# Expert-gate products from f32 to fp32r (gates split high and low, 64 blocks), with an own tile for the expert's activations and a new order of the index stage and of the last experts

## What is computed

```python
s1, s2 = scores of the query halves against keys1, keys2     # 128 keys each
top_s, pos = lax.top_k(v1[..., :, None] + v2[..., None, :], PEER_TOPK)
expert = i1 * PEER_KEYS + i2                # per token 8 heads x 16 experts
gate = softmax(top_s)
z = einsum('cd,ced->ce', x, u[expert])
act = gelu(z) * gate
out = einsum('ce,ced->cd', act, v[expert])
return rmsnorm(x + out, norm_final_g)
```

## Time and profile before

| | us |
|---|---|
| median of 3 runs | 2832.45 (2830.51 to 2834.54) |
| the profiled execution | 2833.08 |
| its span, first to last instruction | 2831.20 |
| TensorE busy | 2763.3 (98%) |
| DVE busy | 1814.0 (64%) |
| ACT busy | 1388.5 (49%) |
| POOL busy | 251.2 (9%) |
| TensorE's granted clock, mean share | 0.99 |
| read from HBM | 501.49 MB |

### The profile page before, as it was taken

One profiled execution on the slowest core, in us unless ns is written; L12 is line 12 of the kernel. 1 busy time (PEld: TensorE's weight loads), 2 busy tenths in 40 slices (PEclk: granted clock), 3 DMA queues, 4 the chain that ended last, 5 costly groups with the idle time before them and its releaser, 6 DMA issues.

```text
span 2831.2 us, 49456 instructions
## 1 busy us (share of the span) xinstructions
PE 2763.3 (98%) x15452; PEld 2414.6 (85%) x15452; DVE 1814.0 (64%) x2892; ACT 1388.5 (49%) x2016; POOL 251.2 (9%) x340
## 2 busy tenths in 40 slices
PE   8999999899999999999999999999999999999998
PEld 6888877788888888889999999888888888888886
DVE  6666655657986666578886666666664555555555
ACT  5454545545665444455555554555544444444444
POOL 0000000000000000000004997000000000000000
PEclk9999999999999999999999999999999999999999
DMA  6544454554554444555565454666665555555555
GB/s 245 188 148 167 159 178 150 169 202 144 172 166 164 156 156 141 181 196 184 185 207 174 159 160 153 219 210 214 210 205 179 193 193 193 192 193 193 193 192 191
DMA packets 153406, 514.70 MB, mean 182 GB/s; under 512 B 17040, under 2 KB 33680, under 8 KB 152208
## 3 DMA queue, kind: packets, MB, share of 16 engines
q1 hardware_dynamic: 131904, 482.54, 51.5%
q10 hardware_dynamic: 21456, 31.60, 3.1%
HBM read 501.49 MB, written 12.58 MB: 182 GB/s over the span
## 4 chain that ended last, share of the span: by engine, by line
PE 59%; DVE 1%; ACT 0%; issue 0%; DVEq 0%; POOL 0%; ACTq 0%; POOLq 0%
PE bank L482 12%; PE bank L2013 8%; PE bank L2014 8%; PE bank L2015 8%; PE bank L487 6%; PE bank L467 3%; PE bank L468 3%; PE bank L469 3%; PE bank L1988 2%; PE bank L522 1%; PE bank L521 1%; PE bank L520 1%; PE bank L1963 0%; DVE act L1027 0%; DVE big L1682 0%
## 5 line engine op out<-in xcount | busy, mean ns | idle before, releaser
L444 DVE TENSOR_TENSOR w_lo<-raw,w_hi 128x1024 fp32r<-128x1024 f32 x904 | 1098.3, 1225 | 827.5 <-ACT w_hi L435 822.7
L435 ACT ACTIVATE w_hi<-raw 128x1024 fp32r<-128x1024 f32 x904 | 953.5, 1059 | 1045.6 <-PE bank L2015 384.3
L482 PE MATMUL bank<-act,w_hi 128*128 128x512 f32 x3072 | 787.7, 398 | 4.5 <-ACT big L797 1.8
L482 PEld LDWEIGHTS bank<-act,w_hi 128*128 128x128 f32 x3072 | 554.4, 189 | 110.9 <-issue 5.5
L487 PEld LDWEIGHTS bank<-act,w_lo 128*128 128x128 f32 x3072 | 418.8, 190 | 31.1
L487 PE MATMUL bank<-act,w_lo 128*128 128x256 f32 x3072 | 427.8, 282 | 0.0
L2013 PE MATMUL bank<-w_hi,act 128*128 128x512 f32 x1024 | 399.5, 390 | 4.9 <-DVE act L1653 4.9
L2014 PE MATMUL bank<-w_lo,act 128*128 128x512 f32 x1024 | 399.1, 390 | 0.0
L2015 PE MATMUL bank<-w_hi,act 128*128 128x512 f32 x1024 | 399.1, 390 | 0.0
L467 PE MATMUL bank<-act,w_hi 128*128 128x256 f32 x912 | 261.6, 287 | 2.3 <-DVE w_lo L444 1.9
L469 PE MATMUL bank<-act,w_lo 128*128 128x256 f32 x912 | 259.4, 284 | 0.0
(11 more groups left out here) (276 smaller groups left out, 2344.8 us busy)
## 6 DMA issues: line engine op xcount, KB each, us to landing
raw<-in_stream SPq DMA_DIRECT2D x904, 512.0 KB, 3.3
big<-in_ukv ACTq DMA_DIRECT2D x16, 512.0 KB, 5.2
z_kept<-cst ACTq DMA_DIRECT2D x64, 128.0 KB, 3.2
cst<-z_kept ACTq DMA_DIRECT2D x64, 128.0 KB, 3.7
big<-in_x SPq DMA_DIRECT2D x2, 1024.0 KB, 9.5
big<-in_rows ACTq DMA_DIRECT2D x2, 1024.0 KB, 5.9
big<-in_rg_w ACTq DMA_DIRECT2D x1, 2048.0 KB, 8.1
x_kept<-big ACTq DMA_DIRECT2D x1, 2048.0 KB, 6.6
```

The source lines that it names most:

```text
L435: act.activation(w_hi[:, s, :], raw[:, s, :], ACT.Copy).then_inc(hi_ready, 1)
L444: dve.tensor_tensor(w_lo[:, s, :], raw[:, s, :], w_hi[:, s, :].bitcast(F32), ALU.subtract).then_inc(lo_ready, 1)
L482: pe.matmul(bank[:, :], w_hi[:, s, kk * P:(kk + 1) * P], act2[:, k, :, :].rearrange("p a n -> p (a n)"), start=(k == 0), stop=False)
```

## The change

- `u_gates` has 64 pairs instead of 32, `u_late` 32 instead of 64. Behind each of the 64 pairs, not behind each unit, stand the gate products of four tokens. `EARLY`, the number of z blocks stored to DRAM, rises from 64 to 96. 32 of them are fetched and multiplied in the late stage, 64 in the first 32 turns of the experts.
- The gate products are fp32r. The one-hot times gate is made twice, once with the gate's high part (rounded to fp32r by ACT into `gate_hi`) and once with the rest (`gate_lo`), both by DVE into `weighted`; two products accumulate. The plain one-hot of POOL is the stationary operand of both.
- DVE's order: both parts of tokens 0 and 1, split of unit 0, both parts of tokens 2 and 3, split of unit 1, `add_halves`. ACT: both splits, low half, one `keep_gates` of four tokens, Gelu, store.
- The experts' split activations get a tile of their own, `expert_act`, laid on the place of `weighted`. Experts 0 and 1 are split before the last late turn. TensorE's unit 0 of the first expert no longer waits for the end of ACT's and DVE's work; unit 1 waits for the last sum.
- Index stage: kw's transposes stand behind the first unit of the first query pair; KID is turned before CKV and copied first, and the scores wait for that copy alone. At the end: scores, rnn inputs of block 0, scores, rnn queries of block 0.
- Last two experts: token tile 0 for both, then tile 1 bank by bank (`last_experts`, `bank_done`). x is fetched early, into `big`. Tile 0 is normed and stored while TensorE works on tile 1. The scaling is shared: DVE one half of the columns, ACT the other after POOL has multiplied it with the gain. Six stores instead of four.

```diff
-         ("wqu", 4 * PH), ("u_decode", 2 * PH), ("u_gates", S // 8), ("u_late", NB // 2), ("v", NB)]
-EARLY = NB // 2
+         ("wqu", 4 * PH), ("u_decode", 2 * PH), ("u_gates", S // 4), ("u_late", NB // 4), ("v", NB)]
+EARLY = 3 * NB // 4
+LATE = NB - EARLY
...
+        with nc.sbuf_tensor("expert_act", [P, 2, 2, S], F32R) as expert_act:
+            pass
+        weighted = sb("weighted", [P, 4, 2, P], F32R)
+        with nc.sbuf_tensor("below_hot", [P, CONST["causal"][0]], F32), \
+                nc.sbuf_tensor("hot", [P, 4, P], F32R) as hot:
+            pass
...
         @block.gpsimd
-                    pool.tensor_scalar(hot[:, 1, s % 4, :], iota, idx8[:, s:s + 1], None, ALU.is_equal)\
+                    pool.tensor_scalar(hot[:, s % 4, :], iota, idx8[:, s:s + 1], None, ALU.is_equal)\
                         .then_inc(hot2, 1)
+            for t in range(TT):
+                pool.wait_ge(y_added, 4 * t + 2)
+                pool.tensor_tensor(OUT[:, t, 0:1024], XF[:, t, 0:1024], final_row[:, 0:1024], ALU.mult)\
+                    .then_inc(gained, 1)
...
         @block.scalar
+            act.wait_ge(ki_turned, 1)
+            act.activation(KIT, banks[2][:, 0:S], ACT.Copy).then_inc(ki_kept, 1)
             for k in range(RT):
...
-            for n in range(2):
-                index_relu(IH // 4 - 1, n)
+            index_relu(IH // 4 - 1, 0)
+            ahead(split_hi, act, "rnn", 0, 2, 0, units=(0,))
+            index_relu(IH // 4 - 1, 1)
...
+            act.activation(gate_hi.bitcast(F32R), slot_t[:, 2, :], ACT.Copy).then_inc(slots_kept, 1)
+            with act.Fori(0, S // 8) as i:
                 for n in range(2):
+                    for u in range(2):
+                        ahead(split_hi, act, "u_gates", i, 2, n, units=(u,))
                     act.wait_ge(unit_done, 2 * pair_of("u_gates", i, 2, n) + 2)
                     act.wait_ge(z_saved[n], i * 16 + (32 * PH + 1))
                     low_half(act, GZ[:, n, :], banks[2 + n])
+                    act.wait_ge(hot_used[3], i * 2 + n + 2)
+                    act.activation(G[:, :, bass.ds(i * 8 + 4 * n, 4)],
+                                   banks[n][:, :].rearrange("p (t b) -> p b t", t=4), ACT.Copy)\
+                       .then_inc(gate_kept[n], 1)
...
         @block.vector
+            step(dve.tensor_tensor(gate_lo, slot_t[:, 2, :], gate_hi, ALU.subtract))
+            step.wait()
+            with dve.Fori(0, S // 8) as i:
                 for n in range(2):
+                    for s in range(4):
+                        tok = i * 8 + (4 * n + s)
+                        dve.wait_ge(hot_used[s], i * 2 + n + 1)
+                        for part, weight in enumerate([gate_hi, gate_lo]):
+                            dve.tensor_scalar(weighted[:, s, part, :], iota, slot_t[:, 0, bass.ds(tok, 1)],
+                                              weight[:, bass.ds(tok, 1)], ALU.is_equal, ALU.mult).then_inc(hot1, 1)
+                        if s % 2:
+                            ahead(split_lo, dve, "u_gates", i, 2, n, units=(s // 2,))
                     add_halves(dve, GZ[:, n, :], banks[2 + n], block_of("u_gates", i, 2, n))
...
+            with dve.Fori(0, (EARLY - LATE) // 2) as i:
                 for n in range(2):
+                    next_expert(i, n)
+                    dve.wait_ge(z_back[n], i * 16 + (8 * LATE + 16))
+                    back = G[:, bass.ds(i * 2 + (LATE + n), 1), :].rearrange("p o n -> p (o n)")
+                    dve.tensor_tensor(back, GB[:, n, :], back, ALU.mult).then_inc(early_ready[n], 1)
...
         @block.tensor
             pe.wait_ge(ckv_kept, 2)
+            index_queries(0, 0, units=(0,))
+            pe.wait_ge(kwt_kept, 1)
+            for t in range(TT):
+                ins = pe.transpose(banks[3][:, t * P:(t + 1) * P], KWT[:, t * P:(t + 1) * P], ident)
+            ins.then_inc(kw_turned, 1)
+            index_queries(0, 0, units=(1,))
+            index_queries(0, 1)
...
+            pe.wait_ge(ki_kept, 1)
...
+            index_scores(IH // 4 - 1, 0)
+            rnn_inputs(0)
+            index_scores(IH // 4 - 1, 1)
+            rnn_queries(0)
...
+            with pe.Fori(0, S // 8) as i:
                 for n in range(2):
                     pe.wait_ge(gelu_ready[n], i + (2 * PH + 1))
+                    halves_out(pe, pair_of("u_gates", i, 2, n), n, banks[2 + n])
+                    pe.wait_ge(gate_kept[n], i + 1)
+                    for s in range(4):
+                        pe.wait_ge(hot1, i * 16 + (8 * n + 2 * s + 2))
+                        pe.wait_ge(hot2, i * 8 + (4 * n + s + 1) + 1)
+                        out_ap = banks[n][:, s * P:(s + 1) * P]
+                        pe.matmul(out_ap, hot[:, s, :], weighted[:, s, 0, :], start=True, stop=False)
+                        pe.matmul(out_ap, hot[:, s, :], weighted[:, s, 1, :], start=False, stop=True)\
+                          .then_inc(hot_used[s], 1)
...
+                    if first and u == 1:
+                        wait_summed(pe, block_of("u_late", LATE // 2 - 1, 2, 1))
...
+            for u in range(2):
+                for n in range(2):
+                    pe.wait_ge(el_ready, NB - 1 + n)
+                    pe.wait_ge(lo_ready, UNITS - 3 + 2 * n + u)
+                    for cc in range(2):
+                        last_experts(0, u, n, cc)
+            for u in range(2):
+                for cc in range(2):
+                    for n in range(2):
+                        last_experts(1, u, n, cc)
```

More of the change, by code:

```diff
@@ L305, in build @@
         final_ready = sem("final_ready")
-        xf_ready = [sem(f"xf_ready{t}") for t in range(TT)]
+        xf_ready = sem("xf_ready")
         x_saved = sem("x_saved")
@@ L833, in rnn_block @@
             def rnn_block(j, first=False):
-                ahead(split_hi, act, "rnn", j, 2, 0, units=(0,))
+                if not first:
+                    ahead(split_hi, act, "rnn", j, 2, 0, units=(0,))
                 act.wait_ge(unit_done, 2 * pair_of("rnn", j, 2, 0) + 2)
@@ new lines, in _, with final_squares @@
+            expert_hi(last * 2 + 2, 0, 2 * pair_of("v", last, 2, 0) + 2)
+            ahead(split_hi, act, "v", last, 2, 1, units=(0,))
+            expert_hi(last * 2 + 3, 1, 2 * pair_of("v", last, 2, 1) + 2)
+            ahead(split_hi, act, "v", last, 2, 1, units=(1,))
+            warm_root()
+            def final_squares(t, cb):
+                cols = slice(cb * 512, (cb + 1) * 512)
+                act.wait_ge(y_added, 4 * t + cb + 1)
+                act.activation(SQ[:, t, cols], XF[:, t, cols], ACT.Square,
+                               accum_out=ss4[:, 4 * t + cb:4 * t + cb + 1]).then_inc(fin_squares, 1)
@@ L1015, in _ @@
+            act.wait_ge(gained, 1)
+            act.wait_ge(fin_rstd, 1)
+            final_scale(0, slice(0, 1024))
+            final_squares(1, 2)
+            final_squares(1, 3)
+            final_root(1)
+            act.wait_ge(gained, 2)
+            act.wait_ge(fin_rstd, 2)
+            for q in range(2):
+                final_scale(1, slice(q * 512, (q + 1) * 512))
         @block.vector
@@ L1382, in _ @@
                     ahead(split_lo, dve, "qi", i, 2, n + 2)
-            for n in range(2):
-                index_sum(IH // 4 - 1, n)
+            index_sum(IH // 4 - 1, 0)
+            ahead(split_lo, dve, "rnn", 0, 2, 0, units=(0,))
+            index_sum(IH // 4 - 1, 1)
             for t in range(TT):
@@ L1423, in rnn_block @@
             def rnn_block(j, first=False):
-                ahead(split_lo, dve, "rnn", j, 2, 0, units=(0,))
                 if not first:
+                    ahead(split_lo, dve, "rnn", j, 2, 0, units=(0,))
                     rnn_gates(j - 1)
@@ L1676, in _ @@
[L1676 to L1684 removed]
+                dve.wait_ge(act_ready[n], LATE // 2 + 1)
@@ new lines, in _, with add_expert_bank @@
+            with dve.Fori((EARLY - LATE) // 2, NB // 2 - 2) as i:
+                for n in range(2):
+                    next_expert(i, n)
+            last = NB // 2 - 2
+            ahead(split_lo, dve, "v", last, 2, 0)
+            expert_lo(last * 2 + 2, 0, last * 2 + 3)
+            ahead(split_lo, dve, "v", last, 2, 1, units=(0,))
+            expert_lo(last * 2 + 3, 1, last * 2 + 4)
+            ahead(split_lo, dve, "v", last, 2, 1, units=(1,))
+            def add_expert_bank(t, cb):
+                dve.wait_ge(bank_done, 4 * t + cb + 1)
+                xs = XF[:, t, cb * 512:(cb + 1) * 512]
+                dve.tensor_tensor(xs, xs, banks[4 * t + cb][:, :], ALU.add).then_inc(y_added, 1)
@@ L1687, in _ @@
+            dve.wait_ge(y_added, 4)
+            dve.wait_ge(final_ready, 16)
+            final_rows(0, slice(1024, 2048))
+            add_expert_bank(1, 2)
+            add_expert_bank(1, 3)
+            final_mean(1)
+            final_reciprocal(1)
+            dve.wait_ge(y_added, 8)
+            for q in range(2):
+                final_rows(1, slice(1024 + q * 512, 1536 + q * 512))
```

(24 more changed lines are left out.)

227 lines of the change are left out of this document (116 added, 111 removed).

## The result

| | us |
|---|---|
| before, median of 5 runs beside it | 2832.55 (2830.51 to 2835.32) |
| after, median of 5 runs | 2848.18 (2846.38 to 2849.47) |
| ratio | 1.0052, 95% interval 1.0038 to 1.0067 |
| span of the profiled execution | 2847.66 (before 2831.20) |

The change makes the kernel 15.6 us slower, where 3.4 us on the profiled execution was forecast. The 2848.18 lies just above the upper end of the whole range, 2848, and 3 us above the forecast's own, 2845. The three gains came about as forecast, one of them larger; the gate part cost 34 us and not 19.6.

A forecast was written before the change was run, and what follows sets the result against it. TensorE, busy 98%, was taken to bound the kernel; gate part +19.6, into the experts -6.8, index end -4.6, index front 0, tail -4.8 give +3.4 us on 2833.08: 2836, range 2812 to 2848, the forecast's own 2827 to 2845.

The forecast's parts named there:

- The three gains: Forecast savings outside the gate part: into the experts -6.8 us, end of the index stage -4.6, tail -4.8.
- The products: Gate stage: each fp32r product of 128 columns costs TensorE 0.111 us, a block 0.93 as before, so fp32r alone brings nothing.
- Rival 2: Gate stage: load isn't the pace, products take 0.07 us, wait for DVE stays, pair 6.76; 2829 us; chance 0.09.
- rival 3: Gate stage: an fp32r product of 128 columns costs 0.22 us, like an f32 pair of records; pair 7.38; 2869; chance 0.08.
- rival 4: Gate stage: two one-hots per token cost DVE 0.07 us more each, 18 us in all; 2854; chance 0.07.
- The chain to the last token: Gate stage: unit 0's end through w_hi, w_lo and four one-hots takes 3.75 us; TensorE, there at 3.47, waits about 0.3.
- what stands behind the wait: Gate stage: loads aren't taken ahead of the wait, so two products and one for the next unit follow it, 0.33 us.
- Rival 1: Gate stage: DVE's last two tokens are in time, no wait, pair 6.53, in all -18.2 us; 2815; chance 0.18.
- Into the experts: Late stage to first expert: own tile lets unit 0 start at once, unit 1 waits some 0.3 us; -6.8 us.
- End of the index stage: Last score groups: rnn block between them removes two Relu-copy waits and the half clock behind; -4.6 us (bounds -3 and -5).
- the zero: Front of the index stage: earlier KIT copy offset by DVE's delayed chain to KID; scores start about 611.5; 0 (bounds -3, +2).
- Tail: Last product to the end: one add left, scaling shared by DVE and ACT; 7.3 us instead of 12.4; -4.8 (bounds -3.5, -5.3).

The follow-up runs named there:

- the first experiment: Changed kernel with DVE making all eight one-hots of a block ahead of the split of unit 0, instead of four ahead and four behind; 2810.66 us, ratio 0.9919.
- two experiments: One-hots-first kernel with both fp32r products per token, pair 6.487 us (2810.66 us), against it without the low parts' products, pair 6.04 (2781.95 us).
- the kernel with no wait: Changed kernel with all eight one-hots of a block ahead of DVE's split of unit 0; 2810.66 us, pair 6.487.
- the longer loop: Changed kernel with TensorE's gate-stage loop written over four pairs instead of two; 2844.50 us, ratio 1.0041.
- the f32 run: Changed kernel's order, but gates not split: one f32 one-hot and one f32 product (two records) per token; 2821.48 us, ratio 0.996.

## Why the prediction was off

**The products: right.** No row showed an fp32r product of 128 columns, and 0.111 was taken from the f32 records of 128 and 64 columns. The trace of after and of the first experiment has 0.11, the difference of two experiments 0.112. Rival 2 (0.07) and rival 3 (0.22) are out. So is rival 4, whose 2854 came nearest to the measured time: the one-hots were not dearer than in the rows but cheaper, 0.257 apart. The 81 ns that the Trainium skill gives for it (TensorE: Matmul & The Clock Gate, Back-to-back issue gap) are not what any run here shows. The section LDWEIGHTS of the same page of the Trainium skill gives the columns of the load divided by 1.2 in ns, 107 for 128 columns; that agrees with the distance of 0.11 for both data types (the record of a load itself covers 0.19).

**The chain to the last token: right to 0.02.** Step by step, the forecast and the medians over the pairs of after:

| step | forecast | measured |
|---|---|---|
| end of unit 0 to `w_hi` | 0.20 | 0.20 |
| to `w_lo` | 1.18 | 1.18 |
| to the first one-hot | 1.15 | 1.14 |
| to TensorE's product of the last token | 1.22 | 1.24 |
| sum | 3.75 | 3.77 |
| to the next pair | 0.33 | 0.27 or 0.60 |
| unit 0 | 2.80 | 2.90 or 2.85 |
| the pair | 6.88 | 6.93 or 7.22 |

With POOL at rest the one-hots stand 0.257 apart and not 0.31, but from the last one's start to the product it is 0.47, of which 0.34 is the one-hot: 0.13 behind it where 0.05 was taken. The two errors cancel.

**The step that failed: what stands behind the wait.** The prediction said "three of them (two products, one for the next unit) stand behind it: 0.33". In every second block it is 0.60. The chain that ended last, in order of time, shows it (start, us, what):

```profile
1708.42 0.08 issue
1708.50 0.32 PE bank L2112
1708.83 0.11 PE bank L2113
1708.94 0.17 issue
1709.10 0.96 PE bank L499 x3
```

The loop on TensorE's queue has two pairs, so after every second block comes its end. The trace has the compare-and-branch there at 1708.62, 208 ns long, and register operations at 1708.88 and 1708.98; the next unit's first product starts at 1709.10. The branch stands in the queue behind the wait for the last token's one-hots, which ends at 1708.41 here; from there to the next unit's first load are 0.69 us, and the products of the last token cover only part of them. In the first experiment, with the same loop, the one-hots are early, the branch comes 0.7 to 1.2 us before the first product of its block, and the distance behind the block is 0.11 every time. The Trainium skill, Advanced Engine Details and Errata, Control Flow Timing, gives about 108 ns for a compare-and-branch; the 31 in TensorE's gate loop that go round take 207 to 215 here, the last one, which leaves it, 76. The second term that was too small is unit 0. It was put at 2.80, the price of a unit behind a unit. Behind a block it takes 2.85 even with no wait (1696.29 to 1699.14 in the first experiment), and 2.90 behind the exposed end of the loop.

In numbers: the pair was 7.08 on average instead of 6.87. 63 x 0.21 = 13.2 us. The start to the end of the first block took 7.86 instead of 7.2, for TensorE stood idle for 0.79 there before the third token (1516.98), whose one-hots came behind `w_lo`; the late stage took 0.6 more. Together 14.5, which is the whole miss of 34.1 - 19.6. The price of the wait thus was 7.08 - 6.487 = 0.59 a pair, 37 us in all, and the first experiment got 37.5 back. By the distances in after the 0.59 are 0.30 of lateness before two tokens, 0.10 in the second records of these two (0.16 apart and not 0.11), 0.16 for 0.33 in every second pair at the end of the loop, and 0.02 in unit 0.

One reading of the prediction was loose, with nothing in the sum hanging on it: the 68 us beside TensorE's busy time are idle time alone. Products at half clock count as busy, as 4.55 of 4.55 at the start of the experts do.

**Rival 1 was the better kernel, not the better forecast.** "No wait" gives 2815 by the prediction's sum; the kernel with no wait took 2810.66, of which 2.7 less are the pair (6.487 for 6.53) and 1.5 the index stage. For the kernel as changed its condition did not hold: the rows' sum of 3.7 against 3.47 was right.

**Into the experts: right.** TensorE goes from the late stage into the first expert with no gap and at full clock:

```profile
2142.09 1.11 PE L504 MATMUL bank<-act,w_lo 128*128 128x256 f32 x8
2143.04 0.40 PE L2138 MATMUL bank<-w_hi,expert_act 128*128 128x512 f32 x1
...
2145.56 0.39 PE L2140 MATMUL bank<-w_hi,expert_act 128*128 128x512 f32 x1
2146.01 0.50 PE L2138 MATMUL bank<-w_hi,expert_act 128*128 128x512 f32 x1
```

The 0.45 at the start of unit 1 is the wait for the last sum, 0.22 over the usual distance, and the product behind it comes 0.1 late as well (2146.01 to 2146.34); 0.3 was forecast.

**End of the index stage: one cause was not seen.** Both waits for the Relu copies and the half clock behind them are gone, as forecast: the last group of scores (660.50) and the rnn unit behind it follow without a gap.

```profile
660.50 1.14 PE L1931 MATMUL bank<-big 64*128 64x256 f32 x8
661.57 1.67 PE L499 MATMUL bank<-act,w_hi 128*128 128x512 f32 x6
```

But before had one more stretch at half clock, right behind the first scores, which the prediction had not read. Windows of before and of after for the same time:

```profile
612.51:615.92 3.41, 3.41 (x17) 3.36 (x16) 1.76 (x4) 1.08 (x2) 0.00 (x0) 0.50 0.39 153
```

```profile
612.51:615.92 3.41, 3.41 (x29) 3.34 (x28) 2.45 (x5) 1.48 (x4) 0.00 (x0) 1.00 0.90 265
```

29 records instead of 17 in the same time are 12 x 0.12 = 1.4 us, the difference between -4.6 and -6.1. TensorE had idled 2.43 in one piece before it; in after it idles 1.52 before the transposes and nothing before the scores.

```profile
610.27 0.44 PE L1949 MATMUL bank<-cst,big 128*128 128x128 f32 x2 [1.52 <-DVE big L1434]
610.55 1.04 PE L1954 MATMUL bank<-cst,big 128*128 128x128 f32 x8
611.51 1.14 PE L1931 MATMUL bank<-big 64*128 64x256 f32 x8
```

The first score itself comes at 611.51, where 611.49 was before: the zero holds, and the wait in front of the transposes is for DVE's KID, the chain that the prediction named. The run with the transposes moved back gains 1.0 there.

**Tail: right.** From the last product to the first output row of DVE 2.33 us (2839.90 to 2842.23), forecast 2.3. POOL's product with the gain, whose price was open between 1.6 and 4.7, took 2.40 for tile 0 and 3.35 for tile 1, and ended 0.88 before ACT's scaling asks for it:

```profile
2838.06 3.35 POOL L628 TENSOR_TENSOR big<-big 128x1024 f32<-128x1024 f32 x1 [2.62 <-DVE big L1766]
```

```profile
2842.23 1.42 DVE L1781 SCALAR_TENSOR_TENSOR big<-big,stat 128x512 f32<-128x512 f32 x2
```

```profile
2842.29 1.33 ACT L1067 ACTIVATE big<-big,stat 128x512 f32<-128x512 f32 x2 [0.29 <-DVE stat L1777]
```

The two scalings of 512 columns take 0.71 each and not 0.61, and the rest up to the end 5.43 us where 5.0 was counted.

**What stays open.** Of the 0.13 between the end of a late one-hot (1708.37) and its product (1708.50) the trace has 0.04 before TensorE's own wait instruction (1708.41) and 0.09 from there to the load, with which the product starts; why it takes so long isn't shown. That the ends of TensorE's and ACT's loops are the 0.21 of the run with f32 products in the changed order is read from its records, not tried. That the tail's, the experts' and the index's gains are each what the table says rests on the traces; only their sum was tried, by the run with the old gate stage.

## What to carry to other kernels

Look at what stands *behind* a wait on the bounding engine, not only at how late its data are: loads that could not be taken ahead and the end of a loop come on top, here as much again as the lateness itself (0.30 late, 0.59 lost). The last data before the end of a loop must even be early, here 0.7 us before the first load behind it, and the loops of the engines that feed it have ends as well. When a producer engine serves two consumers in a fixed order, put first what is ready early: eight one-hots that hang on nothing stood behind a split that could not start before unit 0 had ended, and exchanging them turned 15.6 us lost into 22.4 won, 18.2 of which are the other parts. And splitting an operand in two for cheaper products is worth nothing where each product comes with its own load of 128 columns (here of the same `hot` tile twice): products of 64 and of 128 columns stood 0.11 apart alike, so the load must be what sets the pace.

## What the hardware showed beyond the forecast

- With a load of a stationary tile of 128 columns for each product of 128 columns, one fp32r product and one record of an f32 product both take 0.11 us; the two kernels that differ only in that type have the same pair, 6.487 us.
- The end of a loop on TensorE's queue (compare-and-branch of 208 ns and register operations) costs nothing where the wait for the last one-hots ends 1.7 us or more before the next unit's first load (first experiment), 0.24 us where they are just in time (f32 products in the changed order) and 0.33 us where they are late (after). In the last two the next unit's first load comes 0.68 and 0.69 us behind the wait. ACT's loop end, in the same way, lets `w_hi` start 0.18 us late in the longer loop and 0.27 in the f32 run, when it falls on the moment that ACT waits for.
- A wait of 0.06 and 0.24 us in two places of a block makes the pair 0.59 us longer in all.
